# Buffer addresses, the order of the first transfers, and an early root table in a two-block transformer kernel

## The reference, cut to what matters

```python
for l in range(DEPTH):                                   # first block, DEPTH = 2
    h = hybrid_mixer(x, pos, row, col, w_in[l], ...)     # x @ w_in, attention, gating, @ w_mix_out
    x = layer_norm(ALPHA * x + h, ln1_g[l], ln1_b[l])
    h = memory_cross_attention(x, mem, x_wq[l], x_wkv[l], x_wo[l])
    x = layer_norm(ALPHA * x + h, ln2_g[l], ln2_b[l])
    h = conv_ffn(x, f_w_up[l], f_conv_k[l], f_conv_b[l], f_w_down[l])
    x = layer_norm(ALPHA * x + h, ln3_g[l], ln3_b[l])
for layer in range(DEPTH):                               # second block
    x = sandwich(x, c_act, mixer, ...)                   # even_mixer, then odd_mixer
    x = sandwich(x, c_act, mlp, ...)                     # square(relu(h @ w1)) @ w2
```

## Time and profile before

| | us |
|---|---|
| median of 3 runs (3756.89 to 3759.40) | 3758.27 |
| the profiled execution | 3756.42 |
| its span in the profile | 3754.6 |
| PE busy, share of the span | 3562.8, 95% |
| DVE, ACT, POOL busy | 1604.7, 1013.9, 2072.2 |

### The profile page before, as it was taken

How to read it: one execution, slowest core, us unless ns; L and a number is a source line. 1 busy time by engine, 2 the same in 40 slices (tenths; PEclk the granted TensorE clock), 3 DMA queues, 4 the chain that set the end, 5 groups by cost and what they waited for, 6 DMA issues and landing times.

```text
span 3754.6 us, 44932 instructions
## 1 busy us (share of the span) xinstructions
PE 3562.8 (95%) x17537; PEld 2765.0 (74%) x17537; DVE 1604.7 (43%) x2437; ACT 1013.9 (27%) x1955; POOL 2072.2 (55%) x2138
## 2 busy tenths in 40 slices
PE   8999988999999999889998999997999899989998
PEld 6777776888777777768886666775888677668886
DVE  3564435755336553367553544334322233233222
ACT  2344224212123441332112454333111133211111
POOL 5444563767554446557774554442666544447664
PEclk9999999999999999999998999998999999989999
DMA  4222222665221213236642222221333222123332
GB/s 137 62 63 61 86 86 72 197 184 174 84 73 54 68 43 112 73 114 186 188 128 68 68 67 68 73 59 52 104 95 93 85 69 61 57 62 90 96 91 73
DMA packets 578795, 345.20 MB, mean 92 GB/s; under 512 B 16032, under 2 KB 562073, under 8 KB 578585
## 3 DMA queue, kind: packets, MB, share of 16 engines
q1 hardware_dynamic: 574637, 337.34, 30.8%
q10 hardware_dynamic: 3947, 4.99, 0.4%
HBM read 340.14 MB, written 2.14 MB: 91 GB/s over the span
## 4 chain that ended last, share of the span: by engine, by line
PE 87%; DVE 6%; ACT 4%; issue 1%; DMA 1%; POOL 0%; SPq 0%; ACTq 0%; DVEq 0%
PE gemm L220 24%; PE gemm L223 23%; PE gemm L226 23%; PE scores L300 6%; PE outs L300 6%; PE gemm L255 1%; PE scores L1455 1%; PE gemm L256 1%; PE gemm L257 1%; DMA w_raw<-in_w_in 1%; ACT tiles L633 1%; DVE x_t L1110 0%; DVE tiles L1107 0%; DVE scales L702 0%; ACT tiles L605 0%
## 5 line engine op out<-in xcount | busy, mean ns | idle before, releaser
L199 POOL CAST w_high<-w_raw 128x512 fp32r<-128x512 f32 (+1 forms) x1067 | 698.8, 655 | 1565.8 <-PE gemm L226 1176.8
L201 POOL TENSOR_TENSOR w_low<-w_raw,w_high 128x512 fp32r<-128x512 f32 (+1 forms) x1067 | 1385.2, 1298 | 85.4
L220 PE MATMUL gemm<-x_high,w_high 128*128 128x512 f32 x2584 | 714.0, 398 | 21.5 <-POOL w_high L199 5.4
L223 PE MATMUL gemm<-x_low,w_high 128*128 128x512 f32 x2584 | 694.5, 391 | 0.0
L226 PE MATMUL gemm<-x_high,w_low 128*128 128x512 f32 x2584 | 691.7, 390 | 0.0
L220 PEld LDWEIGHTS gemm<-x_high,w_high 128*128 128x128 f32 x2584 | 474.3, 188 | 129.0 <-issue 18.4
L223 PEld LDWEIGHTS gemm<-x_low,w_high 128*128 128x128 f32 x2584 | 486.0, 188 | 105.0
L226 PEld LDWEIGHTS gemm<-x_high,w_low 128*128 128x128 f32 x2584 | 485.1, 188 | 103.4
L220 PE MATMUL gemm<-split_tiles,w_high 128*128 128x512 f32 (+1 forms) x1456 | 396.3, 392 | 8.4 <-DVE tiles L1545 2.4
L223 PE MATMUL gemm<-split_tiles,w_high 128*128 128x512 f32 (+1 forms) x1456 | 388.2, 387 | 0.0
L226 PE MATMUL gemm<-split_tiles,w_low 128*128 128x512 f32 (+1 forms) x1456 | 386.9, 386 | 0.0
(11 more groups left out here) (342 smaller groups left out, 3605.3 us busy)
## 6 DMA issues: line engine op xcount, KB each, us to landing
w_raw<-in_mlp_w SPq DMA_DIRECT2D x112, 512.0 KB, 4.0
w_raw<-in_mod_w SPq DMA_DIRECT2D x96, 512.0 KB, 3.7
w_raw<-in_w_in SPq DMA_DIRECT2D x88, 512.0 KB, 3.7
w_raw<-in_f_w_up SPq DMA_DIRECT2D x88, 512.0 KB, 4.9
w_raw<-in_e_w_in SPq DMA_DIRECT2D x48, 512.0 KB, 3.9
w_raw<-in_f_w_down SPq DMA_DIRECT2D x32, 512.0 KB, 4.1
w_raw<-in_o_w_in SPq DMA_DIRECT2D x30, 512.0 KB, 3.8
w_raw<-in_w_branch SPq DMA_DIRECT2D x48, 256.0 KB, 2.6
```

What stands on the lines that cost most here:

```text
L199: me.pool.tensor_copy(WH[:, h, 0:n], W32[:, s, c0:c0 + n]).then_inc(sem["w_rounded"], 1)
L201: me.pool.tensor_tensor(WL[:, h, 0:n], W32[:, s, c0:c0 + n], WH[:, h, 0:n].bitcast(F32), ALU.subtract).then_inc(sem["w_split"], 1)
L220: me.pe.matmul(o, WH[:, h, (k - k0) * cols:(k - k0 + 1) * cols], src(k)[0], start=begin and k == 0, stop=False)
L223: me.pe.matmul(o, WH[:, h, (k - k0) * cols:(k - k0 + 1) * cols], src(k)[1], start=False, stop=False)
```

## The change: what it does

Three parts. First, `work`, `split_tiles` and `plain_tiles` are allocated directly behind `mats`, ahead of the small buffers. Second, the order of the first transfers: ACT asks only for the identity (64 KB of `mats`), under a semaphore of its own. SP asks for x, then for the weights of units 16 to 19 ahead of all else (they are handed out later from the list `early`), then for the seventeen small parameters, the other fourteen matrices, `c`, the mask, and the four table transfers. The pair of units 16 and 17 is put ahead of `layer_columns` and of the silu, and PE waits for the other matrices only behind them. Third, `centred_norm` begins with a root of one column on ACT.

```diff
+        T2 = sb("work", [P, 8, S])
+        with nc.sbuf_tensor("split_tiles", [P, RT, S], F32R) as R:
+            pass
+        RF = sb("plain_tiles", [P, RT, S])
         mask = sb("mask", [P, 3 * P])
...
         def fetch(me, w, n, cols):
+
+            if me.early:
+                return me.early.pop(0)
+            return issue_fetch(me, w, n, cols)
...
             moved = []
+            if me.act:
+                me.act.activation(st[:, 60:61], zero[:], ACT.Sqrt)
             if me.dve:
                 me.dve.wait_ge(sem["pe_step"], me.mean_made)
...
+            first_two = unit_pair(me, [zi(16), zi(17)], KD, xs, me.x_ready) if me.x_ready else None
+            if l == 0:
+                layer_columns(me, 0)
+                me.c_ready = me.tick("act_step")
+                if me.act:
+                    me.act.wait_ge(sem["c_landed"], 32)
+                    me.act.activation(c_act, c_act, ACT.Silu).then_inc(sem["act_step"], 1)
+                if me.pe:
+                    me.pe.wait_ge(sem["mats_landed"], 16)
             fresh = me.tick("dve_step")
...
             if me.act:
-                me.act.dma_start(MAT[:], a["mats"]).then_inc(sem["mats_landed"], 16)
-                with nc.allow_non_contiguous_dma(reason="one column of eight"):
-                    me.act.dma_start(c_act, a["c_2"][0].rearrange("(t p) -> p t", p=P)).then_inc(sem["c_landed"], 16)
-                me.act.dma_start(mask[:], a["band"]).then_inc(sem["c_landed"], 16)
-            for part in range(9):
-                layer_rows(me, 0, me.act, part, None)
+                me.act.dma_start(MAT[:, 0, :], a["mats"][:, 0, :]).then_inc(sem["ident_landed"], 16)
+            me.early = [issue_fetch(me, wcols(a["w_in"], 0, 0, KD, n * P), KD * P, P) for n in (16, 17, 18, 19)]
+            for part in (2, 3, 4, 5, 6, 7, 8, 0, 1):
+                if part == 0:
+                    if me.sp:
+                        me.sp.dma_start(MAT[:, 1:len(CONSTS), :],
+                                        a["mats"][:, 1:len(CONSTS), :]).then_inc(sem["mats_landed"], 16)
+                        with nc.allow_non_contiguous_dma(reason="one column of eight"):
+                            me.sp.dma_start(c_act, a["c_2"][0].rearrange("(t p) -> p t", p=P)
+                                            ).then_inc(sem["c_landed"], 16)
+                        me.sp.dma_start(mask[:], a["band"]).then_inc(sem["c_landed"], 16)
+                layer_rows(me, 0, me.sp, part, None)
...
-                        me.pe.wait_ge(sem["mats_landed"], 16)
+                        me.pe.wait_ge(sem["ident_landed"], 16)
```

More of the change, by code:

```diff
@@ L136, in build @@
         st = sb("stats", [P, 64])
-        T2 = sb("work", [P, 8, S])
         scale_rows = sb("scales", [P, P])
@@ L145, in build @@
                  "act_to_pe", "dve_done", "act_done", "pool_done", "in_landed", "dve_to_sp", "out_stored",
-                 "dve_to_pool", "dve_step", "act_step", "pe_step", "params", "tables", "bias_stored", "hankel", "x_landed0", "x_landed1", "mats_landed", "c_landed"]
+                 "dve_to_pool", "dve_step", "act_step", "pe_step", "params", "tables", "bias_stored", "hankel", "x_landed0", "x_landed1", "mats_landed", "ident_landed", "c_landed"]
         sem = {n: ctx.enter_context(nc.semaphore(n)) for n in names}
@@ L163, in __init__ @@
                 self.x_ready, self.x_done = None, 0
+                self.early, self.late = [], None
                 self.sp, self.pool, self.act, self.dve, self.pe = (eng if kind == k else None for k in
@@ L172, in build, with issue_fetch @@
         layer_params = [sb(f"layer_params{l}", [P, 266]) for l in range(DEPTH)]
-        with nc.sbuf_tensor("split_tiles", [P, RT, S], F32R) as R:
-            pass
-        RF = sb("plain_tiles", [P, RT, S])
         def fetch(me, w, n, cols):
+            if me.early:
+                return me.early.pop(0)
+            return issue_fetch(me, w, n, cols)
+        def issue_fetch(me, w, n, cols):
             s = me.loads % WRING
@@ L1189, in rope_turn @@
                 return ready, made
-            first_two = unit_pair(me, [zi(16), zi(17)], KD, xs, me.x_ready) if me.x_ready else None
             if me.pe:
@@ L3018, in program @@
             low_part(KD - 1)
[L3019 to L3023, removed]
-            if True:
-                for l in range(DEPTH):
-                    first_layer(me, l)
+            for l in range(DEPTH):
+                first_layer(me, l)
             from_second(me)
```

## The result

The changed kernel takes 3728.2 us (median of 4 runs, 3724.3 to 3732.5) where the kernel before takes 3757.6 on the same chips: a ratio of 0.9922, with a 95% interval from 0.9905 to 0.9939, which is 29 us less (23 to 36). Forecast were 3722 and a range of 3712 to 3736. The profiled execution took 3724.3, 32.1 less than that of before.

What follows compares the result with a forecast made beforehand. The prediction took TensorE's own rate on the gemm lines as the bound. Gains of 26 (addresses), 7 (start) and 3.6 us (roots), 36.6 in all, took 3758.3 to 3721.7, rounded 3722, with a range of 3712 to 3736.

Steps and rivals of the forecast that it cites:

- The bound: TensorE's own rate on the gemm lines; an edit counts only through the matmul step or PE's waits.
- Part 1, the mechanism: Gemms from `split_tiles`: a start at a multiple of 128 bytes, as `x_high` has, cuts 6.8 ns a matmul.
- If the start address is the cause: Condition for matmuls from `split_tiles`: each then goes from 233.4 to 226.6 ns.
- Part 1, the size: 4032 matmuls of 512 columns from `split_tiles` at 6.8 ns, 27.4 us; taken as 26, bounds 22 and 30.
- `work`: Full float32 matmuls reading this buffer: moving it put at 0 us, between -1 and +1.
- The 256-column matmuls: 384 matmuls for the memory's keys and values: left at nothing, since POOL is busy without a gap between them.
- Part 2: Start of the kernel: first gemm at 15.6 instead of 24.27, unit 18 at 30.8; gain 7 us, bounds 0 and 10.
- Part 3: Roots of `centred_norm`: table load off the path, 2.6 us over both ln1; 3.6 us in all, bounds 2.5 and 5.
- The sum: Whole kernel: 26 + 7 + 3.6 = 36.6 us less, 3722 us; own range 3714 to 3731, chance 0.68.
- rival 2: The start gives nothing: tables land at about 36 to 40, PE waits for gelu as now; 3728.7 us, chance 0.13.

Runs made afterwards that it cites:

- fifth kernel: Kernel before with 96 bytes of padding ahead of `split_tiles`, which then starts at 1396 x 128 in its old region: 1.0012 of before.
- tenth: Changed kernel with 32 bytes of padding ahead of the first buffer, so everything moves together: 3731.2 us, 0.9934 of before.
- fourth kernel: Changed kernel with 32 bytes of padding ahead of `split_tiles` alone: 3746.8 us, 0.9976 of before.
- ninth kernel: Kernel before with 224 bytes of padding ahead of `split_tiles`, in its old region: 0.9951 of before, 18.4 us less.
- the shapes' figures: Matmul groups of six kinds without the model's computation; 256 columns at 0, 32, 64, 128 bytes from the weights: 119.9, 117.8, 113.3, 118.5 ns.
- seventh: Changed kernel with 32 bytes of padding ahead of `x_high` and 96 behind `x_low`: 3786.3 us, 1.0088 of before.
- twelfth: Changed kernel with 208 small unused matmuls added in PE's waits in the norms and ahead of unit pairs: 3702.6 us, 0.9869 of before.
- sixth kernel: Changed kernel with 64 bytes of padding ahead of `split_tiles` alone: 3735.6 us, 0.9954 of before.

## Why the prediction was right, and where it was not

**The bound** was read right: PE's step, and PE's waits. All of the gain lies in these two.

**Part 1, the mechanism.** "If the start address is the cause" held, and 32 bytes undo it. The step that failed is the one ahead of it: that the good place is a multiple of 128 bytes. `x_high` and `split_tiles` differ in that in the earlier trace rows, but they differ as well in their distance from `w_high`, and I did not ask which of the two counts. The fifth kernel (a multiple of 128, 232.8 ns) and the tenth (no multiple of 128, 227.3 ns) decide for the distance, to a multiple of 256. The change came out right since 171648 - 32896, the start of `w_high`, is 542 x 256; with 128 bytes more it would have gained next to nothing, and my argument would have forecast the same 26 us. It was right in number by a rule that is wrong.

**Part 1, the size.** 26 was too much. The fourth kernel and the changed one differ by 18.6 us, by the ratios 20, and the addresses alone gave 16.5. One term was mis-sized and one was missing. 6.8 ns is the difference between two undisturbed stretches; over the whole run it is 233.3 - 227.3 = 6.0, since some 10% of the steps at the good place still take 229 to 240 ns. And the faster gemms come with more long steps than before's 450: 15 in the ninth kernel, 30 in the changed one, 38 in the tenth, 48 with the addresses alone, which is 3 to 10 us that no term of the sum held. An example is this place, first before, at a granted clock of 1.00, then in the changed kernel:

```profile
1927.16 1.19 PE L220 MATMUL gemm<-split_tiles,w_high 128*128 128x512 f32 x4 [0.96 <-DVE x_t L567]
1928.19 1.09 PE L223 MATMUL gemm<-split_tiles,w_high 128*128 128x512 f32 x4
```

```profile
1910.80 1.23 PE L227 MATMUL gemm<-split_tiles,w_high 128*128 128x512 f32 x4 [2.21 <-DVE x_t L574]
1911.84 1.90 PE L230 MATMUL gemm<-split_tiles,w_high 128*128 128x512 f32 x4
1913.54 1.87 PE L233 MATMUL gemm<-split_tiles,w_low 128*128 128x512 f32 x4
```

PE waits 2.21 us for DVE's `x_t` instead of 0.96, and eight steps then take 427 ns. That all the added long steps come about in this way isn't shown, and neither is that the faster gemms cause them: the mean granted clock differs between executions of one kernel too (0.970 to 0.975 in before's).

**`work`** moved for nothing, as forecast: 592 ns against 591. The cost of full float32 doesn't depend on the distance at all (429.1 ns a pass at all four).

**The 256-column matmuls** were left at nothing because POOL is their bound. Their distance went from 32 bytes to 0, by the shapes' figures from 117.8 to 119.9 ns, and in the whole kernel from 117.0 to 119.7. Their steps under 300 ns take 45.5 us in all before and 44.8 after, so nothing of it shows in the time, as the prediction had it.

**Part 2** was right nearly step by step: first gemm 16.34 for 15.6, end of the pair 29.14 for 27.7, from there to unit 18 2.3 us for 2.9, unit 18 at 31.46 for 30.8; 6.3 us for 7, and 5.6 alone. In the kernel with the start alone the tables landed at 30.0, forecast 29.5. What was late is the pair: POOL took 5.2 us for the four steps ahead of it, and eight of its matmuls took 0.43 us each from 17.55 on, where the granted clock was 0.61 (17 to 19 us) and 0.54 (19 to 21 us).

**Part 3** was right: 1.42 us in each ln1 for 1.3, 0.2 in ln2; 5.3 us alone for 3.6, with 3.6 inside the interval.

**The sum.** 36.6 us forecast, 29 measured; the 7 us that are missing are part 1's. By the time alone the forecast isn't borne out: 3728.2 is nearer to rival 2's 3728.7 than to its own 3721.7. What tells them apart is the start, which gave 6.3 us in the trace and 5.6 alone, where rival 2 had none. So the range held since it was wide enough for a start that fails, and it was part 1 that took that room. (Its ends don't quite follow from the bounds either: gains of 45 and of 24.5 us would be 3713.3 and 3733.8.)

Between the profiled executions the difference is 32.1, and there the profile flatters: before's own profiled execution lost 3.3 us to the clock at 2231 to 2238 behind a wait of 1.32 us:

```profile
2230.00:2235.00 5.00, 4.77 (x12) 1.72 (x14) 2.16 (x4) 1.85 (x7) 0.00 (x0) 0.63 0.38 103
```

The kernel with the early root alone has the same wait and stays at 1.00:

```profile
2228.00:2233.00 5.00, 5.00 (x27) 2.78 (x26) 3.18 (x5) 4.39 (x17) 0.00 (x0) 1.00 0.02 7
```

Compared at this place, eight of the eleven other whole kernels gain the same 3.3 us on the profiled execution of before, whatever their change; the seventh gains 1.4, and the tenth and the twelfth nothing. The tenth differs from the changed kernel by 32 bytes of padding alone. So it most likely belongs to the execution and not to the change, though no second trace of before is there to show it.

## What to carry to other kernels

When two buffers stream at different paces, list all in which they differ, their distance from the other operand too, and move one of them alone before a rule is made of it: a buffer moved by 128 bytes told here what the whole change could not. For fp32r matmuls of 512 columns with weights reloaded each time, a multiple of 256 bytes between moving operand and weights was the best place here; with 256 columns it was the worst, so the shape has to be tried. And look at the granted clock behind PE's waits: matmuls without a purpose in those waits were worth 20 to 26 us here, nearly as much as the change.

## What was not expected of the hardware

The pace of an fp32r matmul of 512 columns depends on the distance between the starts of its two operands to a multiple of 256 bytes, in steps from 226.7 (0) over 228.8 (64) and 231.6 (16) to 234.2 ns (160), whether POOL works beside it or not. In full float32 and with 128 columns it doesn't (429.1 and 110.8 ns). With 256 columns the worst of the four distances tried is 0 (119.9 ns by itself, 119.7 in the changed kernel); the best by itself is 64 bytes (113.3), which the sixth kernel, with 117.8, does not bear out.
